# Memory attention's scores and mixes as three single-pass products of high and low parts

## The reference

```python
q = rms_norm(x, g) @ w_q          # 256 tokens x 1024
k, v = mem @ w_k, mem @ w_v       # 256 memory tokens x 1024
s = einsum("qhd,khd->hqk", q, k) * 256 ** -0.5     # scores
p = softmax(s)                                      # shares
x = x + einsum("hqk,khd->qhd", p, v) @ w_o          # mixes, then the output product
```

## Time and profile before

| | |
|---|---|
| median of 3 runs | 1110.7 us (1110.38 to 1110.97) |
| profiled execution, first to last instruction | 1111.3 us |
| TensorE busy | 1092.0 us, 98% |
| VectorE busy | 749.5 us, 67% |
| ScalarE busy | 583.6 us, 53% |
| scores (L2081), both layers | 64 records, 15.0 us busy |
| mixes (L2102), both layers | 64 records, 14.8 us busy |
| HBM read | 193.04 MB |

### The profile page before, as it was taken

One profiled execution on the slowest core, in us unless ns is written; L12 is line 12 of the kernel. 1 busy time (PEld: TensorE's weight loads), 2 busy tenths in 40 slices (PEclk: granted clock), 3 DMA queues, 4 the chain that ended last, 5 costly groups with the idle time before them and its releaser, 6 DMA issues.

```text
span 1111.3 us, 15418 instructions
## 1 busy us (share of the span) xinstructions
PE 1092.0 (98%) x6251; PEld 951.6 (86%) x6251; DVE 749.5 (67%) x1024; ACT 583.6 (53%) x940; POOL 54.4 (5%) x87
## 2 busy tenths in 40 slices
PE   8999999999999999999999999999999999999997
PEld 6799988788898988989988988788988989888986
DVE  5736776865679977555678855546967546788643
ACT  3458653444477775555444544456765545444442
POOL 3311000000010000001000000000011000000000
PEclk9999999999999999999999999999999999999999
DMA  9956464655654325535555555544445435555550
GB/s 343 381 161 207 135 196 162 233 184 189 223 168 126 115 77 189 175 99 149 197 184 184 196 182 196 189 153 151 152 153 189 132 115 190 190 190 189 162 179 38
DMA packets 118776, 195.09 MB, mean 176 GB/s; under 512 B 6586, under 2 KB 39762, under 8 KB 118705
## 3 DMA queue, kind: packets, MB, share of 16 engines
q1 hardware_dynamic: 116144, 187.51, 50.7%
q0 software_dynamic: 2560, 6.60, 2.0%
HBM read 193.04 MB, written 1.05 MB: 175 GB/s over the span
## 4 chain that ended last, share of the span: by engine, by line
PE 83%; DVE 10%; ACT 5%; issue 1%; DMA 1%; POOL 1%; SPq 0%; DVEq 0%; ACTq 0%; POOLq 0%
PE product L669 55%; PE small L706 5%; PE product L706 5%; DVE conv_out L2719 5%; PE product L708 3%; PE small L708 3%; PE product L996 3%; ACT w_high L591 1%; ACT diagonal L2612 1%; DVE w_low L601 1%; PE small L816 1%; PE small L2081 1%; PE small L731 1%; PE small L1462 1%; PE small L1451 1%
## 5 line engine op out<-in xcount | busy, mean ns | idle before, releaser
L601 DVE TENSOR_TENSOR w_low<-w_raw,w_high 128x2048 fp32r<-128x2048 f32 (+3 forms) x160 | 350.0, 2190 | 180.2 <-ACT w_high L591 178.6
L591 ACT ACTIVATE w_high<-w_raw 128x2048 fp32r<-128x2048 f32 (+3 forms) x160 | 292.1, 1832 | 175.9 <-PE product L669 144.2
L669 PE MATMUL product<-w_high,H 128*128 128x512 f32 (+2 forms) x736 | 239.7, 393 | 0.5 <-DVE w_low L601 0.5
L669 PEld LDWEIGHTS product<-w_high,H 128*128 128x128 f32 x736 | 137.9, 188 | 26.9 <-DVE w_low L601 0.9
L669 PE MATMUL product<-H,w_high 128*128 128x256 f32 x816 | 150.9, 283 | 0.1
L669 PE MATMUL product<-w_low,H 128*128 128x512 f32 (+2 forms) x368 | 142.3, 387 | 0.0
L669 PEld LDWEIGHTS product<-H,w_high 128*128 128x128 f32 x816 | 126.6, 188 | 1.1 <-DVE w_low L601 0.5
L669 PE MATMUL product<-H,w_low 128*128 128x256 f32 x408 | 114.2, 280 | 0.0
L706 PE MATMUL product<-H,w_high 128*128 128x512 f32 x256 | 89.1, 391 | 0.0
L706 PE MATMUL small<-H,w_high 128*128 128x512 f32 x256 | 89.1, 391 | 0.0
L669 PEld LDWEIGHTS product<-w_low,H 128*128 128x128 f32 x368 | 69.3, 188 | 11.9 <-issue 0.2
(11 more groups left out here) (412 smaller groups left out, 1784.3 us busy)
## 6 DMA issues: line engine op xcount, KB each, us to landing
w_raw<-in_ffn_w_gate SPq DMA_DIRECT2D x20, 1024.0 KB, 5.0
w_raw<-in_ffn_w_up SPq DMA_DIRECT2D x20, 1024.0 KB, 5.0
w_raw<-in_ffn_w_down SPq DMA_DIRECT2D x20, 1024.0 KB, 5.0
w_raw<-in_w_merge SPq DMA_DIRECT2D x16, 1024.0 KB, 5.2
w_raw<-in_w_ada SPq DMA_DIRECT2D x32, 256.0 KB, 6.5
w_raw<-in_mem_w_k SPq DMA_DIRECT2D x8, 1024.0 KB, 5.0
w_raw<-in_mem_w_v SPq DMA_DIRECT2D x8, 1024.0 KB, 5.0
w_raw<-in_conv_w_pw SPq DMA_DIRECT2D x16, 512.0 KB, 4.7
```

The source lines that it names most:

```text
L591: k.act.eng.activation(parts_of(k, i, j)[0], raw_of(k, i), ACT.Copy).then_inc(*k.act.tells("weights_high", ("weights high", i)))
L601: k.vec.eng.tensor_tensor(low, raw, high.bitcast(F32), ALU.subtract).then_inc(*k.vec.tells("weights_low", ("weights low", i)))
L669: mm = pe.eng.matmul(bank[:, off:off + wide], a, r, start=b not in started, stop=True, skip_group_check=True)
```

## The change

Scores and mixes are made of parts too. ScalarE writes high parts of type float32r, VectorE low parts, and each float32 matmul becomes three float32r ones.

- Keys and values of a layer are split whole: one ScalarE copy and one VectorE subtraction of 128x2048 each for keys and for values. They stand in steps 1 (keys) and 2 (values) of the product that adds the mixer's output to x, each behind that step's chunk. The low parts replace `mem_keys` and `mem_values` in place; the high parts lie where `HN` and the gains lie, which are not in use then.
- A head's queries: the copy that was there writes the high part, a subtraction of 128x512 on VectorE is added. The scores wait for it.
- A head's turned shares: the same, the low part lies in the upper half of the query operand `H.low`, which has been used up by then. The mixes wait for it.
- Two VectorE subtractions stand behind the chunk before the tops of heads 0 and 1 (queries 0 and 1); four (queries 2, shares 0 and 1, queries 3) between a chunk and the tops of head 2; two (shares 2 and 3) between the shares of head 3 and the second output chunk.

```diff
+def act_split_memory(k, layer, what):
+    of, high = (k.mem_keys, k.keys_high) if what == "keys" else (k.mem_values, k.values_high)
+    k.act.wait_ge(k.act.last, (f"mem {what}", layer))
+    k.act.eng.activation(high[:, :, :], of[:, :, :], ACT.Copy).then_inc(*k.act.tells("memory_high", (f"{what} high", layer)))
+
+def vec_split_memory(k, layer, what):
+    of, high, low = (k.mem_keys, k.keys_high, k.keys_low) if what == "keys" else (k.mem_values, k.values_high, k.values_low)
+    k.vec.wait_ge((f"{what} high", layer))
+    k.vec.eng.tensor_tensor(low[:, :, :], of[:, :, :], high[:, :, :].bitcast(F32), ALU.subtract).then_inc(
+        *k.vec.tells("memory_low", (f"{what} split", layer)))
+
+SPLIT_MEMORY = {1: "keys", 2: "values"}
...
-def vec_add_to_x(k, key, norm):
+def vec_add_to_x(k, key, norm, layer=None):
     for step in range(4):
         if step == 3:
             for t in range(NT):
                 vec_add(k, (key, t), ("products", key, 2), norm, 0, t)
         vec_chunk(k)
+        if layer is not None and step in SPLIT_MEMORY:
+            vec_split_memory(k, layer, SPLIT_MEMORY[step])
...
 def pe_memory_scores(k, layer, h):
-    pe.wait_ge(("mem q", layer, h), ("mem keys", layer), k.small.before((key, "scores")))
+    pe.wait_ge(("mem q", layer, h), ("keys split", layer), k.small.before((key, "scores")))
...
-            mm = pe.eng.matmul(bank[:, t * S:(t + 1) * S], k.q_mem[:, kt, t * P:(t + 1) * P], k.mem_keys[:, kt, :],
-                               start=t == 0 and j == 0, stop=True, skip_group_check=True)
+            for n, (q, keys) in enumerate(((k.q_low, k.keys_high), (k.q_high, k.keys_low), (k.q_high, k.keys_high))):
+                mm = pe.eng.matmul(bank[:, t * S:(t + 1) * S], q[:, kt, t * P:(t + 1) * P], keys[:, kt, :],
+                                   start=t + j + n == 0, stop=True, skip_group_check=True)
...
 def pe_memory_mix(k, layer, h):
-    pe.wait_ge(("turned rows", key), ("mem values", layer), k.small.before((key, "mixed")))
+    pe.wait_ge(("shares split", key), ("values split", layer), k.small.before((key, "mixed")))
...
-            mm = pe.eng.matmul(bank[:, f * S:(f + 1) * S], k.mem_values[:, j, c:c + P], p[:, j * S:(j + 1) * S],
-                               start=f == 0 and j == 0, stop=True, skip_group_check=True)
+            for n, (values, p) in enumerate(((k.values_low, high), (k.values_high, low), (k.values_high, high))):
+                mm = pe.eng.matmul(bank[:, f * S:(f + 1) * S], values[:, j, c:c + P], p[:, j, :],
+                                   start=f + j + n == 0, stop=True, skip_group_check=True)
...
+def vec_memory_q(k, layer, h):
+    V, (high, low, ps) = k.vec, memory_q_views(k, layer, h)
+    V.wait_ge(("mem q high", layer, h))
+    V.eng.tensor_tensor(low, ps, high.bitcast(F32), ALU.subtract).then_inc(
+        *V.tells("memory_q_low", ("mem q", layer, h), k.product.free((("mem q", layer, h // 2), h % 2))))
...
+def vec_memory_turned(k, layer, h):
+    V, key = k.vec, ("mem", layer, h)
+    high, low = shares_parts(k, layer, h)
+    V.wait_ge(("shares high", key), k.turned.before(key))
+    V.eng.tensor_tensor(low, k.small.of((key, "turned"))[:, :].rearrange("p (j n) -> p j n", n=S), high.bitcast(F32), ALU.subtract).then_inc(
+        *V.tells("turned_low", ("shares split", key), k.small.free((key, "turned"))))
...
 def vec_memory(k, layer):
...
+    vec_memory_q(k, layer, 0)
+    vec_memory_q(k, layer, 1)
     vec_chunk(k)
     vec_memory_tops(k, layer, 0)
     vec_memory_tops(k, layer, 1)
     vec_memory_shares(k, layer, 0)
     vec_memory_shares(k, layer, 1)
     vec_chunk(k)
+    vec_memory_q(k, layer, 2)
+    vec_memory_turned(k, layer, 0)
+    vec_memory_turned(k, layer, 1)
+    vec_memory_q(k, layer, 3)
     vec_memory_tops(k, layer, 2)
...
     next(out)
     vec_memory_shares(k, layer, 3)
+    vec_memory_turned(k, layer, 2)
+    vec_memory_turned(k, layer, 3)
     next(out)
...
```

More of the change, by code:

```diff
@@ L394, in layout @@
                 slots.append(self.sb(f"{name}{i}", [P, CK * CN + more], F32R))
-        self.X, self.HN = self.sb("X", [P, NT, D]), self.sb("HN", [P, NT, D])
+        self.X = self.sb("X", [P, NT, D])
+        self.parts_at = self.at
+        self.HN = self.sb("HN", [P, NT, D])
         self.gains_at = self.at
@@ L468, in layout_second @@
         self.rotated = self.ring("rotated", 2, [P, 4 * DH * ROT // 2])
+        keys_at = self.at
         self.mem_keys, self.mem_values = self.sb("mem_keys", [P, KT, S]), self.sb("mem_values", [P, NT, D])
@@ L483, in layout_second @@
         self.memory_rings = self.ring("mrows", 3, [P, 512]), self.ring("mturned", 2, [P, 512])
-        self.q_mem = self.sb("q_mem", [P, KT, S])
         self.to_line()
+        self.q_high = self.sb("q_high", [P, KT, S], F32R)
         o = self.pair("o_mem", KT)
+        self.q_low = self.sb("q_low", [P, KT, S], F32R)
+        self.keys_high, self.values_high = self.sb("keys_high", [P, KT, S], F32R, self.parts_at), self.sb("values_high", [P, NT, D], F32R, self.parts_at + 4 * KT * S)
+        self.keys_low, self.values_low = self.sb("keys_low", [P, KT, S], F32R, keys_at), self.sb("values_low", [P, NT, D], F32R, keys_at + 4 * KT * S)
         self.o_mem = [Operand(f"o_mem{layer}", o) for layer in range(2)]
@@ L856, in pe_add_to_x, with act_add_to_x @@
         yield
-def act_add_to_x(k, norm):
+def act_split_memory(k, layer, what):
[8 more added lines that the diff above has]
+SPLIT_MEMORY = {1: "keys", 2: "values"}
+def act_add_to_x(k, norm, layer=None):
     for step in range(4):
         act_chunk(k)
+        if layer is not None and step in SPLIT_MEMORY:
+            act_split_memory(k, layer, SPLIT_MEMORY[step])
         if step == 3:
@@ L2096, in pe_memory_mix @@
     key, pe = ("mem", layer, h), k.pe
-    bank, p = k.small.take((key, "mixed")), k.turned.of(key)
-    pe.wait_ge(("turned rows", key), ("mem values", layer), k.small.before((key, "mixed")))
+    bank, (high, low) = k.small.take((key, "mixed")), shares_parts(k, layer, h)
+    pe.wait_ge(("shares split", key), ("values split", layer), k.small.before((key, "mixed")))
     for f in range(MHT):
@@ L2104, in pe_memory_mix, with memory_q_views @@
     mm.then_inc(*pe.tells("mixed", ("mixed", key), k.turned.free(key)))
+def memory_q_views(k, layer, h):
+    at = slice(2 * h, 2 * h + 2)
+    return k.q_high[:, at, :], k.q_low[:, at, :], k.product.of((("mem q", layer, h // 2), h % 2))[:, :].rearrange("p (k n) -> p k n", n=S)
 def act_memory_q(k, layer, h):
[L2108 to L2111, removed]
+    A, (high, _, ps) = k.act, memory_q_views(k, layer, h)
+    A.wait_ge(("products", ("mem q", layer, h // 2), 1))
+    A.eng.activation(high, ps, ACT.Copy).then_inc(*A.tells("memory_q", ("mem q high", layer, h)))
@@ new lines, in vec_memory_q, with shares_parts @@
+def vec_memory_q(k, layer, h):
[3 more added lines that the diff above has]
+        *V.tells("memory_q_low", ("mem q", layer, h), k.product.free((("mem q", layer, h // 2), h % 2))))
+def shares_parts(k, layer, h):
+    high = k.turned.of(("mem", layer, h))[:, :].bitcast(F32R).rearrange("p (j n) -> p j n", n=S)
+    return high, k.H_mem[layer].low[:, CK + h % 2 * 2:CK + h % 2 * 2 + 2, :]
@@ new lines, in act_memory_turned @@
+def act_memory_turned(k, layer, h):
+    A, key = k.act, ("mem", layer, h)
+    k.turned.take(key)
+    A.wait_ge(A.last, ("turned", key), k.turned.before(key))
+    A.eng.activation(shares_parts(k, layer, h)[0], k.small.of((key, "turned"))[:, :].rearrange("p (j n) -> p j n", n=S), ACT.Copy).then_inc(
+        *A.tells("turned_rows", ("shares high", key)))
+def vec_memory_turned(k, layer, h):
[4 more added lines that the diff above has]
+        *V.tells("turned_low", ("shares split", key), k.small.free((key, "turned"))))
@@ L2128, in turned @@
     def turned(h):
-        act_turn_rows(k, ("mem", layer, h), 2 * S)
+        act_memory_turned(k, layer, h)
     act_chunk(k)
@@ L2677, in act_conv @@
     A.ended("conv")
-    drain(act_add_to_x(k, k.norms["mem", 0]))
+    drain(act_add_to_x(k, k.norms["mem", 0], 0))
     A.wait_ge(*k.all_ended("conv"))
@@ L2784, in vec_conv @@
     V.ended("conv")
-    drain(vec_add_to_x(k, "pw2", k.norms["mem", 0]))
+    drain(vec_add_to_x(k, "pw2", k.norms["mem", 0], 0))
     V.wait_ge(*k.all_ended("conv"))
@@ L3047, in fill @@
             out(k, 1, n)
-        project = act_add_to_x(k, k.norms["mem", 1])
+        project = act_add_to_x(k, k.norms["mem", 1], 1)
         for half in range(2):
@@ L3128, in fill @@
         yield from vec_chunks(k, 8)
-        project = vec_add_to_x(k, "diff out", k.norms["mem", 1])
+        project = vec_add_to_x(k, "diff out", k.norms["mem", 1], 1)
         for half in range(2):
```

## The result

Measured: 1112.45 us (median of 17 runs, 1111.30 to 1116.48) against 1110.76 us of the kernel before on the same chip. The ratio is 1.0016, with a 95% interval of 1.0009 to 1.0023, or about 1.8 us more, within the 0.2% that the prediction calls no change. A second set of 11 runs on another occasion gave 1111.51 against 1110.74, ratio 1.0009 (0.9999 to 1.0019). 64 float32 products were replaced, and no time was won.

What follows compares the result with a forecast made beforehand. TensorE, busy 98%, was taken as the bound, with a chain of waits through the memory stage. 0.45 + 1.92 - 2 x 0.18 - 2 x 0.66 = +0.7 us on 1110.7 gave 1111.4 us, range 1109.0 to 1113.3.

Steps and rivals of the forecast that it cites:

- the named signs: Wrong if transposes are not waited for, scores or mixes take much over 1.4 us, or the stages' clock falls under 1.
- the chain: Memory stage: waits leave TensorE at head 2's tops, cross VectorE and ScalarE, return at the output product; 5.75 us, untouched.
- three products of one float32 product: Scores and mixes: three single-pass products take 0.35 us instead of 0.431, saving 0.081 on each of 64, 5.2 us of TensorE.
- transposes of layer 0: Ahead of layer 0's memory stage: values' subtraction delays the addition to x, so transposes start 0.45 us later.
- transposes of layer 1: Ahead of layer 1's memory stage: VectorE has no gap left, the addition to x ends late, 1.92 us lost.
- wait ahead of scores 2: Memory stage: scores 2 wait for the subtraction of queries 2, leaving TensorE idle about 0.55 us.
- output product, layer 0 and layer 1: End of the chain in each memory stage: the output product starts 0.18 us earlier in each layer.
- idle ahead of the output product: Memory stage of both layers: TensorE idle 1.9 us before the output product, where it was 0.6.
- mixes 2 and 3, a layer: Inside the output product, where TensorE sets the time: each goes from 1.73 to 1.40 us, 0.66 less a layer.
- The rival: New idle stretches lower TensorE's clock; a fall costs 1.7 us: one gives 1113.1, three 1116.5; chance 0.18.
- all copies hide: VectorE and ScalarE keep up everywhere, the whole 5.2 us is saved: 1105.5 us, or 1109.0 for half; chance 0.13.
- the products are not single-pass: Scores and mixes: new products run as two records each, adding 55 us over 64 products: 1166 us; chance 0.01.

Runs made afterwards that it cites:

- experiment 1: Changed kernel with the values' split moved from the product ahead of the memory stage into that stage: 1109.29 us, ratio 0.9984 to the kernel before.
- experiment 2: Kernel before with the splits of keys and values added but unused, scores and mixes still float32: 1114.91 us, ratio 1.0036; again 1113.95 us.
- experiment 3: Changed kernel with ScalarE's copy of the attended output's second half moved ahead of the weight chunk's copy: 1110.46 us, ratio 0.9994 to the kernel before.
- experiment 4: Changed kernel with both edits, values' split moved into the memory stage and attended half copied ahead of the chunk: 1106.33 us, ratio 0.9958 to the kernel before.
- experiment 7: Kernel before, without the change, with only the attended output's second half copied ahead of the chunk: 1108.81 us, ratio 0.9985.
- experiment 8: Side by side again: changed kernel with values' split moved and attended half copied first, 1106.20 us; kernel before with only that copy order, 1109.05 us.

## Why the prediction was right, point by point

The forecast was 1111.4, no change within 0.2%, because the products save TensorE time where it does not set the end and the splits cost time where VectorE does. Both halves are shown by experiments 1 to 4: three of them take waits away, and experiment 2 adds the splits without the products. The prices come back within about half a us. Against 1111.5, the change's level in the runs with a mean clock of 0.999, experiment 1 gains 2.2 where the two waits cost 2.7, the lowest run of experiment 3 gains 3.1 where the waits ahead of the output product are 1.63 a layer, and both edits together gain 5.3.

That the first median stayed within the 0.2% is in part luck: 1112.45 holds 1 us of slower runs that the sum does not have, and more of them would have carried it out. Two of the named signs also came out the wrong way: a granted clock under 1 did appear in the stages, by which the prediction would have called itself wrong, and the chain leaves TensorE earlier than expected. Neither touches the terms of the sum.

| term | forecast, us | shown, us |
| --- | --- | --- |
| three products of one float32 product | 0.431 to 0.35 | 0.36 (2.88 / 8) |
| transposes of layer 0 | +0.45 | +0.56 |
| transposes of layer 1 | +1.92 | +2.10 |
| wait ahead of scores 2 | 0.55 | 0.71 (bracket 0.54) |
| output product, layer 0 and layer 1 | -0.18 each | -0.16, -0.18 |
| idle ahead of the output product | 1.9 | 1.63 (bracket 1.47) |
| mixes 2 and 3, a layer | -0.66 | -0.58 |
| sum | +0.7 | +1.2 |

The shown delays are differences of starts between the two traces, less the offset that an execution brought along. The wait ahead of scores 2 and the idle time ahead of the output product are not terms of the sum.

**The transposes.** Right, in place and releaser. They are 0.11 and 0.18 larger. VectorE's end released the transposes 0.14 us later (854.04 against 853.90 in layer 1), where 0.05 was taken from a neighbouring handover; that is 0.09 of each. The rest of layer 1's is VectorE's queue, which ran 0.08 later than forecast.

**The price of a product.** Right in kind, a little too good: 0.071 is saved a product, not 0.081, because three products follow each other in 0.36 and not in 0.35. Over 64 that is 0.6 us. The Trainium skill's four passes for true FP32 (FP8 and Floating Point Precision, section TensorE Precision Notes) would by estimate have promised 0.108, a quarter of 0.431; the runs put the float32 product at 3.6 single passes of 0.12.

**The memory stage.** Right: scores 2 wait for the split, the chain of 5.7 us stands, and it is mostly mixes 2 and 3 that gain. The idle time ahead of the output product was forecast as 1.9 and is shown as 1.47 by the bracket. The forecast took TensorE's end from start-to-start times, while the last record's end lies 0.16 us later (it starts at 483.47 and lasts 0.28, where products follow each other in 0.12); the dearer product explains the rest (scores 2 to scores 3 take 5.85 from start to end, 477.74 to 483.59, where 5.60 was forecast). The end does not depend on it. The wait ahead of scores 2 was 0.16 larger than forecast, since the forecast took the old start of scores 2 from the chain (479.13), while TensorE's timeline has 478.96. And the chain was expected to leave TensorE at the tops of head 2 as before; it leaves at the tops of head 1. That changes no number, because VectorE's chunk (474.72 + 2.29) and ScalarE's copy of queries 2 (476.36 + 0.60), for which the split waits, end within 0.1 us of each other.

**The clock.** The rival had 0.18, for the mechanism that new idle stretches bring a fall. The change's first median, 1112.45, lies 1.0 above the forecast, and in the profiled execution a fall stood exactly where the rival put it. The mechanism is not shown by this, and not excluded either. Against it: the kernel before has such falls in mid-program too, the same program kept its clock at that place in another execution, and filling the idle time hardly moved the medians (1112.13 against 1111.51, 1113.71 against 1113.95). Of the five falls in the profiled executions two stood behind the idle time (854.6 and 855.0) and two, at 188.2 and 189.0, behind 3.4 us in which TensorE was busy throughout; in the kernel before:

```profile
185.60:189.00 3.40, 3.40 (x22) 2.85 (x22) 2.54 (x4) 2.37 (x3) 0.00 (x0) 1.00 0.77 222
```

For it speaks the count of slower runs, those 1.5 us or more above the median that the same program has at a mean clock of 0.999. Of the kernels with the wait of layer 1 (the change, the splits alone, experiment 3) they are 25 of 56, of those without it (the kernel before, experiments 1, 4, 7 and 8) 28 of 134, and of the two with the wait filled 3 of 22. This leans towards the rival. It is no proof: the sets were run on different chips, and nine of the 25 belong to experiment 3, whose level rests on one run and whose profiled fall stood elsewhere. Without that experiment it is 16 of 44.

Where the mean granted clock is 0.999, the change's runs have a median of 1111.5 in both sets (8 each), and the kernel before 1110.5 to 1110.7: the change itself costs about 0.9 us, between the forecast 0.7 and the 1.2 of the table. The rest of the first median, 1 us, is left to the share of slower runs in that set. What sets a fall off stays open. The Trainium skill's warning (TensorE: Matmul & The Clock Gate, section HAM oscillation) about idle gaps between bursts neither failed nor was confirmed here: two falls of five stood behind a gap, and the runs do not show that closing it prevents one.

**The other rivals.** That all copies hide was wrong by the four waits above. That the products are not single-pass is excluded by 282 to 289 ns a record and 0.12 us from start to start.

## What to carry to other kernels

On an engine that is busy for 98% a saving counts only between the waits it has, so follow the chain from the place of the saving to its next return and ask what else is in it: here it was another engine's copy of 1.9 us, of no urgency, standing between two halves of an operand. Put new preparatory work by the slack of the engine that does it, not by the place where its source is at hand; the same split cost 2.7 us of TensorE's waits in one place and none that the profile shows in the stage behind it. And when a change that should pay does not, run the neighbouring edit alone on the kernel before as well: it tells which of the two earned the gain.

## What was not expected of the hardware

- The idle time in a bracket understates what a wait costs on TensorE. 0.60 was worth 0.85 (experiment 7), 0.41 was worth 0.56, 0.54 was worth 0.71, and 1.94 was worth 2.10; the records of pipelined matmuls overlap (at 256 columns 0.28 us long, 0.12 apart). Prices of waits are better taken from start to start.
- Ahead of its last ten microseconds the granted clock fell in 5 of the 13 profiled executions, once in each, at 18.5, 188.2, 189.0, 854.6 and 855.0 us, for 3.4 us or 6.8. Three of these five programs were profiled twice, and the other execution had none. With an estimated 1.7 us for 3.4 at half speed, it is as large as what was to be measured. Even medians of 11 and 17 runs differed by 0.9 us without any cause in the code (1111.51 and 1112.45 for the change), those of 5 and 11 by 1.0 (1114.91 and 1113.95 for the splits alone).
